# A float32r decoder trunk: the two token tiles of a weight unit taken in turn, product by product

## What is computed

```
x = x + 1/2 * SwiGLU_1(RMSNorm(x))                 # 1024 -> 2 x 2816 -> 1024
z = RMSNorm(x) @ mix_w_in                          # 1024 -> 2048, split among four mixers
x = x + concat(y_A, y_B, y_C, y_D) @ mix_w_out     # short conv, spatial gating, 31-tap conv, pooling
x = x + CrossAttn_4heads(RMSNorm(x), RMSNorm(mem)) # 256 memory rows
x = x + 1/2 * SwiGLU_2(RMSNorm(x))
```

## Time and profile before

| | |
|---|---|
| median of 3 runs | 1160.99 us (1160.02 to 1161.08) |
| span of the profiled execution | 1157.8 us |
| instructions | 15216 |
| PE busy | 1130.1 us, 98% |
| weight loads (PEld) busy | 934.1 us, 81% |
| DVE busy | 683.3 us, 59% |
| ACT busy | 568.2 us, 49% |
| mean granted TensorE clock | 0.996 |

### The profile page before, as it was taken

How to read it: one execution, slowest core, us unless ns; L and a number is a source line. 1 busy time by engine, 2 the same in 40 slices (tenths; PEclk the granted TensorE clock), 3 DMA queues, 4 the chain that set the end, 5 groups by cost and what they waited for, 6 DMA issues and landing times.

```text
span 1157.8 us, 15216 instructions
## 1 busy us (share of the span) xinstructions
PE 1130.1 (98%) x5194; PEld 934.1 (81%) x5194; DVE 683.3 (59%) x753; ACT 568.2 (49%) x627; POOL 29.0 (3%) x27
## 2 busy tenths in 40 slices
PE   5999999999999999999999999999999999999996
PEld 4888888888888888888878888888888888888885
DVE  5555545699754555554555555458986446555545
ACT  5544434654555454443455444347464555454433
POOL 2000000000000000000000000000000000000000
PEclk9999999999999999999999999999999999999998
DMA  8655554753652466554555655565455435555451
GB/s 272 200 182 181 181 191 149 236 176 123 206 180 97 135 193 191 186 192 164 180 178 183 192 182 177 182 200 183 146 182 172 139 126 182 181 182 188 166 200 45
DMA packets 158929, 202.67 MB, mean 175 GB/s; under 512 B 6842, under 2 KB 114950, under 8 KB 158864
## 3 DMA queue, kind: packets, MB, share of 16 engines
q1 hardware_dynamic: 156636, 200.85, 53.1%
q10 hardware_dynamic: 2228, 1.01, 0.3%
HBM read 200.79 MB, written 1.05 MB: 174 GB/s over the span
## 4 chain that ended last, share of the span: by engine, by line
issue 96%; POOL 2%; DMA 1%; SPq 0%; DVE 0%; ACTq 0%; DVEq 0%; POOLq 0%; ACT 0%
POOL rstd L364 2%; DMA w_raw<-in_ffn_w_in 1%; SPq L285 0%; DMA poolw_all<-in_pool_w 0%; DVE xs L1105 0%; DVEq L109 0%; SPq L277 0%; POOL poolw L376 0%; ACT w_hi L397 0%; ACTq L434 0%; ACTq L430 0%; SPq L275 0%; SPq L278 0%; POOL par L375 0%; POOLq L363 0%
## 5 line engine op out<-in xcount | busy, mean ns | idle before, releaser
L722 DVE TENSOR_TENSOR w_lo<-w_raw,w_hi 128x2048 fp32r<-128x2048 f32 x194 | 434.7, 2247 | 256.2 <-ACT w_hi L397 256.0
L397 ACT CAST w_hi<-w_raw 128x2048 fp32r<-128x2048 f32 x194 | 363.3, 1873 | 132.6 <-PE acc L1164 124.0
L1162 PE MATMUL acc<-w_hi,xT_hi 128*128 128x512 f32 x896 | 356.4, 398 | 3.4 <-DVE xT_lo L743 2.6
L1164 PE MATMUL acc<-w_hi,xT_lo 128*128 128x512 f32 x896 | 351.0, 392 | 0.0
L1163 PE MATMUL acc<-w_lo,xT_hi 128*128 128x512 f32 x896 | 350.8, 391 | 0.0
L1162 PE MATMUL acc<-w_hi,hT_hi 128*128 128x512 f32 x608 | 241.0, 396 | 0.9 <-DVE hT_lo L876 0.9
L1164 PE MATMUL acc<-w_hi,hT_lo 128*128 128x512 f32 x608 | 237.2, 390 | 0.0
L1163 PE MATMUL acc<-w_lo,hT_hi 128*128 128x512 f32 x608 | 236.8, 389 | 0.0
L1162 PEld LDWEIGHTS acc<-w_hi,xT_hi 128*128 128x128 f32 x896 | 169.2, 189 | 37.5 <-DVE xT_lo L743 3.0
L1164 PEld LDWEIGHTS acc<-w_hi,xT_lo 128*128 128x128 f32 x896 | 169.2, 189 | 35.9
L1163 PEld LDWEIGHTS acc<-w_lo,xT_hi 128*128 128x128 f32 x896 | 169.4, 189 | 33.6
(11 more groups left out here) (103 smaller groups left out, 482.0 us busy)
## 6 DMA issues: line engine op xcount, KB each, us to landing
w_raw<-in_ffn_w_in SPq DMA_DIRECT2D x176, 512.0 KB, 4.6
w_raw<-in_ffn_w_out SPq DMA_DIRECT2D x80, 512.0 KB, 4.5
w_raw<-in_mix_w_in SPq DMA_DIRECT2D x32, 512.0 KB, 4.2
w_raw<-in_xattn_wkv SPq DMA_DIRECT2D x32, 512.0 KB, 4.4
w_raw<-in_mix_w_out SPq DMA_DIRECT2D x16, 512.0 KB, 4.5
w_raw<-in_xattn_wq SPq DMA_DIRECT2D x16, 512.0 KB, 4.7
w_raw<-in_xattn_wo SPq DMA_DIRECT2D x16, 512.0 KB, 4.3
w_raw<-in_ffn_w_out SPq DMA_DIRECT2D x16, 256.0 KB, 2.7
```

The lines of the kernel that those rows point to most:

```text
L397: act.copy(w_hi[:, u % SLOTS, 0:n], w_raw[:, u % SLOTS, 0:n]).then_inc(w_split_hi, 1)
L722: dve.tensor_tensor(w_lo[:, u % SLOTS, 0:n], w_raw[:, u % SLOTS, 0:n], w_hi[:, u % SLOTS, 0:n].bitcast(F32), ALU.subtract).then_inc(w_spli ...
L1162: pe.matmul(o, hi, wh, start=(first and j == 0), stop=False)
L1164: ins = pe.matmul(o, lo, wh, start=False, stop=(last and j == nk - 1))
```

## The change

Units without a hook take the two tiles in turn: for each block `j` the product hi x w_hi of tile 0, then of tile 1, then hi x w_lo of both, then lo x w_hi of both. Successive products go to the two banks of the pair by turns, and each block of weights is streamed for both tiles in a row. The order of the sums in each bank is the same. Tile 0's `unit_done` is raised by the last product but one of the unit, tile 1's by the last one. Units with a hook keep their order. The numbers of products, loads, semaphores and DMAs don't change, and no other engine's program changes. The rest of the diff moves line numbers (fourteen empty lines at the head are gone).

```
-                for t in range(T):
-                    if before:
-                        before(t)
-                    for j in range(nk):
-                        hi = s_hi[:, k0 + j, t * P:(t + 1) * P]
-                        ...
-                        pe.matmul(o, hi, wh, start=(first and j == 0), stop=False)
-                        pe.matmul(o, hi, wl, start=False, stop=False)
-                        ins = pe.matmul(o, lo, wh, start=False, stop=(last and j == nk - 1))
-                    ins.then_inc(unit_done, 1)
-                    if between:
-                        between(t)
+                o = [acc[pair][t][:, :] for t in range(T)]
+                if before or between:
+                    ...
+                    return
+                for j in range(nk):
+                    wh = w_hi[:, slot, j * GN:(j + 1) * GN]
+                    wl = w_lo[:, slot, j * GN:(j + 1) * GN]
+                    hi = [s_hi[:, k0 + j, t * P:(t + 1) * P] for t in range(T)]
+                    lo = [s_lo[:, k0 + j, t * P:(t + 1) * P] for t in range(T)]
+                    for t in range(T):
+                        pe.matmul(o[t], hi[t], wh, start=(first and j == 0), stop=False)
+                    for t in range(T):
+                        pe.matmul(o[t], hi[t], wl, start=False, stop=False)
+                    for t in range(T):
+                        ins = pe.matmul(o[t], lo[t], wh, start=False, stop=(last and j == nk - 1))
+                        if j == nk - 1:
+                            ins.then_inc(unit_done, 1)
```

More of the change, by code:

```diff
@@ new lines, in unit @@
+                if before or between:
+                    for t in range(T):
+                        if before:
+                            before(t)
+                        for j in range(nk):
+                            hi = s_hi[:, k0 + j, t * P:(t + 1) * P]
+                            lo = s_lo[:, k0 + j, t * P:(t + 1) * P]
+                            wh = w_hi[:, slot, j * GN:(j + 1) * GN]
+                            wl = w_lo[:, slot, j * GN:(j + 1) * GN]
+                            pe.matmul(o[t], hi, wh, start=(first and j == 0), stop=False)
+                            pe.matmul(o[t], hi, wl, start=False, stop=False)
+                            ins = pe.matmul(o[t], lo, wh, start=False, stop=(last and j == nk - 1))
+                        ins.then_inc(unit_done, 1)
+                        if between:
+                            between(t)
+                    return
```

## The result

The changed kernel takes 1167.33 us (median of 4 runs, 1166.66 to 1167.79) against 1161.03 us for the kernel before (4 runs): a ratio of 1.0059, 95% interval 1.0046 to 1.0071. It is 6.3 us slower; 6.8 us slower was forecast.

A forecast was written before the change was run, and what follows sets the result against it. TensorE, busy 98%, was taken as the bound: products times their 0.2267 us spacing. Zero bank gain plus stalls of 4.6 + 1.1 + 1.1 = 6.8 us gave 1167.8 us, range 1164.0 to 1171.5.

The forecast's parts named there:

- Part 1: Reordered units' 3840 products: changing PSUM bank does not shorten a product, so zero gain.
- Rival (a): Faster: the single bank costs something; at 0.215 us a product 37 us faster, 1124 us; chance 0.05.
- The hidden delays: Tile 0's later end costs nothing where another unit follows; unhidden, 44 FFN chunks would cost 18 us.
- The six turns: Ends of FFN 1, mixer and attention outputs, both layers: next unit 0.77 us late each, 4.6 us.
- rival (d): The second turn at each stage end is late too: 6 x 0.3 us more, 1169.6 us; chance 0.07.
- The end of the kernel: Last update chain and the output DMA behind it start later: 1.1 us.
- the layer's end: End of layer 0: VectorE's chain through the loop's return starts 5 products later and all moves: 1.1 us.
- TensorE's wait for xT_lo: Sign at the layer's end: this wait grows from 2.6 to 3.1 us.
- Rival (c): Slower through the clock: longer idles cost one or two more half-speed spells, 1169.4 or 1171 us; chance 0.12.
- The seven idles: Sign: TensorE's turn newly waits for VectorE's update of tile 0, 7 times, 0.6 to 0.7 us each.
- Rival (b): No change within 0.2%: TensorE's existing waits absorb the stalls, all of it leaving 1.9 us, 1163 us; chance 0.08.

The follow-up runs named there:

- ends_kept: The changed kernel, but the last unit of each stage goes tile by tile, 3696 products staying in the new order: 1160.90 us, ratio 1.0001.
- split_last_after: The changed kernel with the weight subtraction between the two layer-end updates moved behind the variance: 1161.73 us, ratio 1.0011 to the kernel before.
- split_last: The kernel before with the weight subtraction between the two layer-end updates moved behind the variance: 1156.13 us, ratio 0.9964.
- ends_only: The kernel before with only the last unit of each stage alternating tiles, 144 products in the new order: 1168.23 us, ratio 1.0062.
- last_block: The changed kernel, but in each reordered unit's last block tile 0's three products precede tile 1's: 1163.62 us, ratio 1.0026 to the kernel before.
- layer_ends_only: The kernel before with only FFN 2's last unit of each layer alternating tiles: 1163.14 us, ratio 1.0027.
- load96: The kernel before, with the second product of each three loading and multiplying 96 of 128 tokens: 1176.1 us, one run.

## Why the prediction was right, and where it was off

**Part 1 (zero gain from the bank) held.** 0.2267 us a product before and after, and ends_kept at 1.0001. Rival (a) is gone: the 1.8 ns a product from which it would have decided the sign are six times what the experiment leaves room for. The one change of bank per unit in the trace of before had been enough to tell it. The far end of the range for (a) had a weak source: the 0.215 us of the earlier trace rows are for products of 256 columns of float32, another kind, and nothing shows them to be a floor for 512 columns of float32r. The Trainium skill (TensorE: Matmul & The Clock Gate, section "Wait — 56ns, not 53.3ns?") gives 215.7 ns for 512 columns at the full clock, a number that this kernel's products don't reach with one bank or with two.

**The hidden delays were hidden.** ends_kept has them all, 44 FFN chunks among them, and is level with the kernel before.

**The six turns were right to 0.01 us.** 0.77 us each was forecast. In the trace of the change the time from a stage's last product to the next stage's first is 1.36 us at each of the six, against 0.58 before. Three make 2.31, and the stretch in layer 0 grew by 2.36; in layer 1 split_last_after's exceeds split_last's, neither having a spell at half clock, by 2.3. The terms inside also held: VectorE 0.03 us behind tile 0's end, 0.69 us for the update, 0.05 us to TensorE. The experiment with three products ahead of the end showed the term to be linear, 0.33 us a turn where 0.32 was worked out. The second turn was not late (0.59 us from the product ahead of it to the one behind it, 0.58 before), so rival (d) fell.

**The end of the kernel was right:** 11.36 us from the start of the last product to the end in all three traces, 10.23 before.

**The traces' total was closer than their parts, by luck.** The first traces are 7.1 us apart, where 6.8 was forecast. The weak term is the layer's end, with the 3.57 us of the loop's return taken as a constant. The chain up to the variance moved by the 1.13 us of the sum. The idle time behind it is 3.57 to 5.15 us in the traces tile by tile and 4.99 to 5.43 in those with alternating ends. On the means of three traces it is 0.7 us longer with alternating ends, which makes the 1.8 in place of 1.1 us of the table; the ranges overlap, so whether the order has a part in it is not shown. TensorE's wait for xT_lo, forecast as 2.6 -> 3.1 us, is 2.6 to 4.3 in the first group and 4.5 to 4.9 in the second for the same reason. Beside it the start came out 1.7 us shorter in these traces, which no part of the change reaches, and which other kernels of both orders contradict. In the two first traces the start was 2.3 us off the forecast, the layer's end 1.9 us the other way, and the stretch behind it 0.6. They made up for each other, and the total alone would have shown none of it. What carries the sum is not that total but ends_only, last_block and the chain of 1.13 us in every trace.

The 3.2 us between the profiled span and the median of the kernel before are not all time around the span. Every run on record is some 1.7 us longer than its own span; the rest is that the profiled execution was quicker than the median run. The forecast of 6.8 us doesn't hang on it.

**Rival (c), the clock, came true in part at most.** The wait at the layer's end is followed by a spell at 1.2 GHz in every trace of both kernels, and it lasted longer in two of the three with alternating ends. The windows after, against the earlier trace rows:

```profile
595.00:600.00 5.00, 3.63 (x9) 2.86 (x10) 3.08 (x7) 4.71 (x4) 0.00 (x0) 0.50 0.01 3
600.00:605.00 5.00, 5.00 (x21) 4.09 (x20) 4.08 (x4) 2.27 (x4) 0.00 (x0) 0.89 0.42 124
```

Here the clock is still low beyond 600 us; in before it was up again by then (0.68 as the mean of 595 to 600), and in the second trace of the change too (1.00 in 600 to 605). The number of steps of 0.43 us there is 7, 6 and 6 tile by tile, and 9, 5 and 12 with alternating ends. On the means that is 0.5 of the 0.6 us by which the fourth stretch exceeds its three turns. The length of the spell doesn't simply follow TensorE's idle time ahead of it. The spell was short after 2.6, 3.9, 4.3 and 4.5 us, and longer after 4.5 (layer_ends_only), 4.7 and 4.9; but last_block has 4.6 us and a short one (6 steps), and load96, tile by tile, has 3.8 us and a long one (12). After 0.9 us (split_last) and 0.8 (split_last_after) there was none. So it is not shown that the new order lengthens the spell. The seven idles of 0.6 us didn't lower the clock once. The Trainium skill (TensorE: Matmul & The Clock Gate, section "A second HAM failure mode: psum-queue depth-cycling") tells of bank cycling with short idles between groups that makes the clock swing. Here that found nothing to act on: ends_kept changes banks at nearly every product, with no idle between them, and its clock is 0.996 like before.

**Rival (b) fell.** The waits that might have absorbed the stalls are unchanged in the list after (1.3 and 0.9 us).

## What to carry to other kernels

An order that interleaves two results finishes the first one later; it costs nothing while a unit of other work stands between result and reader, and the full update plus handover where a stage ends and the next instruction needs that first result. A single place in the old trace where the supposed condition changes (here the one change of bank per unit) prices such an idea before it is built. And at such an end look at what stands between the two readers on the other engine: one subtraction moved from between them was worth 4.6 us, where the new order gained nothing.

## What the runs showed of the hardware

- Alternating PSUM banks product by product has no effect on the spacing of 128x128 by 128x512 float32r products: 0.2267 us both ways. At the half clock they are 0.427 us apart.
- VectorE's return to the head of its loop took 3.6 to 5.4 us without an instruction, from one execution to the next. The Trainium skill (Runtime: NRT & Kernel Launch, section "Instruction fetch mechanics") says that a taken branch to code outside the window at hand must wait for a fetch of it; these traces fit, and show a spread of 1.9 us: within that idle time three transfers of the DMA kind "instruction" (0.02 MB) start in the trace of before and in that of the change. That they are what VectorE waits for is not shown. Work that was queued ahead of the branch took nothing in split_last: with the 2.29 us subtraction the way from the variance to `xg` was 3.2 us.
- GpSimd's 128x2 power took 2.69 us beside a VectorE subtraction with two SBUF inputs that had started 0.15 us ahead of it, and 0.69 us without one. The Trainium skill (SBUF — State Buffer, section "SBUF: two separate sides") describes an exclusive lock between these two engines for such operations; the two rows agree.
- Loading 96 instead of 128 stationary columns for one product in three made all steps longer (by 2 to 5 ns, +15 us in all; one run). No reason was found.
